# Sparse attention, compressed branch: the weighing of values by one plain fp32 product, or by rounded halves in two

## What is computed

```python
def nsa_attention(h, w_in, ...):
    ...
    n_cmp = (seq - CMP_LEN) // CMP_STRIDE + 1
    v_cmp = compress(vc_blk, pe_v, cv_w1, cv_w2)
    ...
        s_c = jnp.einsum("bgrtd,bgnd->bgrtn", qn, k_cmp) * scale
        p_c = masked_softmax(s_c, cmp_end[None, :] <= pos[:, None])
        o_c = jnp.einsum("bgrtn,bgnd->bgrtd", p_c.astype(v_cmp.dtype), v_cmp)
    ...
        return gt[..., 0:1] * o_c + gt[..., 1:2] * o_s + gt[..., 2:3] * o_w
```

## Time and profile before

| | |
|---|---|
| median of 3 executions | 2837.31 us (2834.18 to 2837.42) |
| the profiled execution | 2838.05 us, its span 2836.3 us |
| TensorE busy | 2756.7 us, 97% |
| VectorE busy | 1632.0 us, 58% |
| ScalarE busy | 1191.4 us, 42% |
| POOL busy | 239.7 us, 8% |
| granted TensorE clock, mean | 0.994 |

### The profile page before, as it was taken

The page is one execution under the profiler, slowest core; times in us unless marked ns, Lnnn a source line. Parts: engine busy times, 40 slices in busy tenths (PEclk is TensorE's granted clock), DMA queues, the critical chain, the costliest instruction groups (busy, mean ns, idle before and its releaser), DMA issues.

```text
span 2836.3 us, 34122 instructions
## 1 busy us (share of the span) xinstructions
PE 2756.7 (97%) x11756; PEld 2076.8 (73%) x11756; DVE 1632.0 (58%) x2240; ACT 1191.4 (42%) x1920; POOL 239.7 (8%) x246
## 2 busy tenths in 40 slices
PE   8999999999999989999999999999988999999999
PEld 6777776888877656888876667888866555788887
DVE  4444336777245766777338975554366666555532
ACT  4333234444234554444336654333234666433321
POOL 0000030000000003000005800000000333000000
PEclk9999999999999999999999999999999999999999
DMA  4222232333323112333231213333333000233323
GB/s 146 75 75 74 77 93 76 89 96 94 91 82 90 52 45 74 89 96 96 87 91 47 66 56 93 95 90 93 94 97 102 27 16 23 82 92 93 96 89 96
DMA packets 421253, 229.35 MB, mean 81 GB/s; under 512 B 8036, under 2 KB 413613, under 8 KB 421037
## 3 DMA queue, kind: packets, MB, share of 16 engines
q1 hardware_dynamic: 418700, 224.39, 27.2%
q10 hardware_dynamic: 2464, 3.81, 0.4%
HBM read 226.07 MB, written 2.10 MB: 80 GB/s over the span
## 4 chain that ended last, share of the span: by engine, by line
PE 85%; DVE 8%; ACT 4%; issue 2%; POOL 1%; DMA 0%; ACTq 0%; DVEq 0%; POOLq 0%
PE lin L815 22%; PE lin L817 22%; PE lin L816 22%; PE att L1126 1%; PE lin L1178 1%; PE att L1010 1%; DVE w_both L2197 1%; PE att L974 1%; PE att L973 1%; PE att L975 1%; ACT w_both L1525 1%; POOL con_p L776 1%; PE lin L1166 1%; PE stat L837 1%; PE trp L1143 1%
## 5 line engine op out<-in xcount | busy, mean ns | idle before, releaser
L2197 DVE TENSOR_TENSOR w_both<-raw,w_both 128x1024 fp32r<-128x1024 f32 x423 | 523.4, 1237 | 551.6 <-ACT w_both L1525 537.3
L815 PE MATMUL lin<-xh,w_both 128*128 128x512 f32 x1856 | 744.2, 401 | 10.3 <-DVE w_both L2197 10.0
L816 PE MATMUL lin<-xl,w_both 128*128 128x512 f32 x1856 | 735.8, 396 | 0.0
L817 PE MATMUL lin<-xh,w_both 128*128 128x512 f32 x1856 | 735.5, 396 | 0.0
L1525 ACT ACTIVATE w_both<-raw 128x1024 fp32r<-128x1024 f32 x423 | 448.2, 1059 | 664.5 <-PE lin L817 574.4
L815 PEld LDWEIGHTS lin<-xh,w_both 128*128 128x128 f32 x1856 | 349.5, 188 | 105.3 <-issue 20.1
L816 PEld LDWEIGHTS lin<-xl,w_both 128*128 128x128 f32 x1856 | 349.6, 188 | 87.0 <-issue 3.4
L817 PEld LDWEIGHTS lin<-xh,w_both 128*128 128x128 f32 x1856 | 349.6, 188 | 85.8
L815 PE MATMUL lin<-ffn_hi,w_both 128*128 128x512 f32 x704 | 280.1, 398 | 0.0
L817 PE MATMUL lin<-ffn_hi,w_both 128*128 128x512 f32 x704 | 279.1, 396 | 0.0
L816 PE MATMUL lin<-ffn_lo,w_both 128*128 128x512 f32 x704 | 279.1, 396 | 0.0
(11 more groups left out here) (450 smaller groups left out, 3759.4 us busy)
## 6 DMA issues: line engine op xcount, KB each, us to landing
raw<-in_ffn_w_up SPq DMA_DIRECT2D x176, 512.0 KB, 3.8
raw<-in_ffn_w_down SPq DMA_DIRECT2D x64, 512.0 KB, 3.8
raw<-in_a_w_in SPq DMA_DIRECT2D x48, 512.0 KB, 3.8
raw<-in_ffn_w_down SPq DMA_DIRECT2D x32, 384.0 KB, 3.3
raw<-in_conv_w_pw SPq DMA_DIRECT2D x24, 512.0 KB, 3.9
raw<-in_nsa_w_in SPq DMA_DIRECT2D x21, 512.0 KB, 3.7
raw<-in_a_w_out SPq DMA_DIRECT2D x16, 512.0 KB, 3.9
raw<-in_w_kv SPq DMA_DIRECT2D x16, 512.0 KB, 3.8
```

What stands on the lines that cost most here:

```text
L815: pe.matmul(bank, w_hi[s][:, k, :], h, start=start and k == 0, stop=False)
L816: pe.matmul(bank, w_hi[s][:, k, :], l, start=False, stop=False)
L817: done = pe.matmul(bank, w_lo[s][:, k, :], h, start=False, stop=stop and k == kc - 1)
L2197: dve.tensor_tensor(w_lo[s][:, :, :], raw[s][:, :, :], w_hi[s][:, :, :].bitcast(F32), ALU.subtract).then_inc(lo_done[s], 1)
```

## The change

The turned compressed weights and the compressed values are each split into a rounded high half and the rest. Of weights `w = wh + wl` and values `v = vh + vl` the products `vh wh`, `vh wl` and `vl wh` are made. The first two share one matmul: `pct` now has `wh` in its rows 0 to 61 and `wl` in rows 64 to 125 (`VC_LOW` = 64), and `vc_hh` has `vh` at both places; the rows 62 and 63 between are cleared. The third is a matmul of 62 rows with `vc_lo`, which lies in the memory of `x_sum`. ScalarE writes `wh` where it wrote the plain copy, and `vh` twice; VectorE makes `wl` (`compressed_low`, in its step 4 of each pair, behind the rotation) and once `vl`. TensorE waits for both writers of `pct` (`n_pc` counts two a pair). VectorE frees the bank of the compressed values, which ScalarE did.

```diff
--- before.py
+++ after.py
@@ -136,6 +136,8 @@
 NPARAM = _at
 PARAM_TILES = (NPARAM + P - 1) // P
 
+
+VC_LOW = 64
 
 CONST_AT = {}
 _at = 0
@@ -236,6 +238,7 @@
         xh = sb("xh", [P, DC, T], F32R)
         xl = sb("xl", [P, DC, T], F32R)
         dif_sm = sb("dif_sm", [P, 32])
+        x_sum_at = -(-nc.sbuf_base // 32) * 32
         x_sum = sb("x_sum", [P, T])
 
         def c_(name):
@@ -353,7 +356,7 @@
         v_all = m.place("v_all", [P, TB, 2, NG * HD])
         kc_bd = m.place("kc_bd", [P, NG, 2 * NCMP])
         vc_pre = m.place("vc_pre", [P, NG, 2 * NCMP])
-        vc_bd = m.place("vc_bd", [2 * NCMP, NG, P])
+        vc_hh = m.place("vc_hh", [VC_LOW + 2 * NCMP, NG, P], F32R)
         gates = m.place("gates", [P, TB, 3 * NH])
         n_raw = m.place("n_raw", [P, 2, T])
         n_t = m.place("n_t", [P, 2, T])
@@ -378,7 +381,8 @@
         n_e = m.place("n_e", [P, 2, 2, T])
         n_pt = m.place("n_pt", [P, 2, TB, T])
         ce = m.place("ce", [P, 2, TB, 2 * NCMP])
-        pct = m.place("pct", [2 * NCMP, T])
+        pct = m.place("pct", [VC_LOW + 2 * NCMP, T], F32R)
+        vc_lo = nc.alloc_sbuf_tensor_at("vc_lo", [2 * NCMP, NG, P], F32R, offset=x_sum_at)
         n_max, n_den, n_inv = (n_sm[:, k:k + 2 * s].rearrange("p (s h) -> p s h", h=2) for k, s in ((0, 2), (4, 2), (8, 3)))
 
         def n_exp(n, hh, w):
@@ -1151,10 +1155,12 @@
                     done.then_inc(n_tc, 1)
 
                 def weigh_compressed(p, bo):
-                    pe.wait_ge(n_pc, p + 1)
+                    pe.wait_ge(n_pc, 2 * p + 2)
                     if p == 0:
-                        pe.wait_ge(n_vcb, 1)
-                    pe.matmul(lin[bo][:, :], vc_bd[:, p // 2, :], pct[:, :], start=True, stop=False)
+                        pe.wait_ge(cleared, 4 + 2 * run[4])
+                        pe.wait_ge(n_vcb, 3)
+                    pe.matmul(lin[bo][:, :], vc_hh[:, p // 2, :], pct[:, :], start=True, stop=False)
+                    pe.matmul(lin[bo][:, :], vc_lo[:, p // 2, :], pct[0:2 * NCMP, :], start=False, stop=False)
 
                 def dense(k, unit, bank, hi, lo, last_pair=False):
                     (us, ut), (ub, ubt) = unit, bank
@@ -1902,9 +1908,10 @@
 
                 exps(0)
                 act.wait_ge(n_vct, 1)
-                act.activation(vc_bd[:, :, :], lin[vc_bank][0:2 * NCMP, :].rearrange("p (g n) -> p g n", g=NG), ACT.Copy).then_inc(n_vcb, 1)
-                act.wait_ge(n_vcb, 1)
-                act.sem_inc(bank_free[vc_bank], 1)
+                act.wait_ge(cleared, 4 + 2 * run[4])
+                for half in range(2):
+                    act.activation(vc_hh[half * VC_LOW:half * VC_LOW + 2 * NCMP, :, :],
+                                   lin[vc_bank][0:2 * NCMP, :].rearrange("p (g n) -> p g n", g=NG), ACT.Copy).then_inc(n_vcb, 1)
                 exp_compressed(0)
                 for p in range(NH // 2):
                     last_pair = p == NH // 2 - 1
@@ -1934,7 +1941,7 @@
                             act.wait_ge(n_tc, p + 1)
                             if p:
                                 act.wait_ge(n_pv, 2 * p - 1)
-                            act.activation(pct[:, :], lin[bo][0:2 * NCMP, :], ACT.Copy).then_inc(n_pc, 1)
+                            act.activation(pct[0:2 * NCMP, :], lin[bo][0:2 * NCMP, :], ACT.Copy).then_inc(n_pc, 1)
                     before = bo
                 place(8 * (NH // 2) - 1)
                 high_out(NH // 2 - 1, before)
@@ -2542,6 +2549,8 @@
 
                 dve.memset(kc_bd[:, :, :], 0.0).then_inc(cleared, 1)
                 dve.memset(vc_pre[:, :, :], 0.0).then_inc(cleared, 1)
+                dve.memset(vc_hh[VC_LOW // 2:VC_LOW, :, :].bitcast(F32), 0.0).then_inc(cleared, 1)
+                dve.memset(pct[VC_LOW // 2:VC_LOW, :].bitcast(F32), 0.0).then_inc(cleared, 1)
                 dve.tensor_scalar(q_gain[:, 0:1], col("nsa_q_norm_2"), HD ** -0.5, None, ALU.mult).then_inc(q_g, 1)
                 dve.wait_ge(rs_ready, rss.next())
                 for n in range(2):
@@ -2618,11 +2627,11 @@
                 scaled_out(g_raw[:, :], n_gr, 1)
                 split_next()
                 s, t = split_next()
-                b, _t = banks.take()
+                vc_bank, _t = banks.take()
                 dve.wait_ge(unit_done[s], t + 1)
                 for half in range(2):
                     r = slice(half * HD, half * HD + HD)
-                    done = dve.tensor_copy(vc_pre[r, :, half * NCMP:(half + 1) * NCMP], lin[b][r, 0:NC].rearrange("p (g n) -> p g n", g=NG))
+                    done = dve.tensor_copy(vc_pre[r, :, half * NCMP:(half + 1) * NCMP], lin[vc_bank][r, 0:NC].rearrange("p (g n) -> p g n", g=NG))
                 done.then_inc(n_vc, 1)
 
                 unseen = n_tabs[:, 2 * T + TB * NP32:].rearrange("p (b n) -> p b n", b=TB)[:, :, 0:NCMP]
@@ -2669,6 +2678,11 @@
                     dve.wait_ge(n_cg, p + 1)
                     dve.tensor_tensor(eights(p), eights(p), c_den.unsqueeze(2).broadcast_to([P, 8, NCMP]), ALU.mult).then_inc(n_cw, 1)
 
+                def compressed_low(p, bo):
+                    dve.wait_ge(n_pc, 2 * p + 1)
+                    dve.tensor_tensor(pct[VC_LOW:VC_LOW + 2 * NCMP, :], lin[bo][0:2 * NCMP, :], pct[0:2 * NCMP, :].bitcast(F32),
+                                      ALU.subtract).then_inc(n_pc, 1)
+
                 def low_out(p, bo):
                     dve.wait_ge(n_o, p + 1)
                     dve.tensor_tensor(att_lo[:, p, :], lin[bo][:, :], att_hi[:, p, :].bitcast(F32), ALU.subtract).then_inc(n_lo, 1)
@@ -2682,6 +2696,11 @@
                 dve.reciprocal(gates[:, :, :], gates[:, :, :]).then_inc(n_gate, 1)
                 top(1)
                 compressed_top(0)
+                dve.wait_ge(n_vcb, 2)
+                dve.tensor_tensor(vc_lo[:, :, :], lin[vc_bank][0:2 * NCMP, :].rearrange("p (g n) -> p g n", g=NG),
+                                  vc_hh[0:2 * NCMP, :, :].bitcast(F32), ALU.subtract).then_inc(n_vcb, 1)
+                dve.wait_ge(n_vcb, 3)
+                dve.sem_inc(bank_free[vc_bank], 1)
                 dve.wait_ge(n_gate, 2)
                 for p in range(NH // 2):
                     last_pair = p == NH // 2 - 1
@@ -2705,7 +2724,9 @@
                                 rotated_q(p + 1)
                             if i == 7:
                                 compressed_top(p + 1)
-                    bo, _t = banks.take()
+                        if i == 4:
+                            bo, _t = banks.take()
+                            compressed_low(p, bo)
                     before = bo
                 low_out(NH // 2 - 1, before)
                 residual_out(1, None, final, ("ffn_norm_g_2", DC))
```

## The result

The changed kernel takes 2849.97 us (median of 5 runs, 2849.6 to 2851.5); the kernel before takes 2837.31 (5 runs, 2834.18 to 2838.21). The ratio is 1.0047 [1.0037, 1.0058]: 12.7 us slower. The direction is the one that was forecast. The size is not: 7.7 us was forecast, and the time lies 1 us above the range.

The account below looks back on a forecast made before the run. TensorE, busy 97% of the span, was taken to bound the kernel. Six pairs at 1.02 us (6.1), pair 6 (2.2) and pair 7 (-0.6) sum to 7.7, on 2837.3 giving 2845.0 us; range 2838.5 to 2849.0.

Parts of the forecast that it names:

- What bounds and where the wait comes: Attention pairs: TensorE bounds; the subtraction queued behind VectorE's rotation makes it wait about 1.3 us, about 2.4 in pair 6.
- VectorE's terms: Subtraction behind the rotation: start 0.72 us after the last rotation instruction's start, 0.69 long, TensorE restarting 0.06 later.
- The choice between 0.61 and 0.72: Subtraction's start behind that of L2604: 0.61 us if unheld, 0.72 if the changed output partition holds it; 0.72 taken.
- TensorE's terms: Two products replacing the plain one: 0.33 + 0.23 + 0.09 us after the wait; TensorE alone saves 0.59 a pair.
- rival 3: Clock falls in the new waits: once gives 2846.5 us, in all seven pairs 2855.5; chance of the many 0.04.
- Pair 6: No dense product ahead of L1157, so TensorE arrives early and the first weighing comes 2.2 us later.
- Cover for others: VectorE's added 0.7 us delays a reciprocal and a maximum, but POOL and ScalarE have enough cover: cost 0.
- the once-only work: Extra rounding copy, low half of the values, bank release and two clearing instructions fall into idle time: cost 0.
- Rival 1: Between L1178 and the next L1157 other waits absorb about half the delay: +3.9, 2841.2 us; chance 0.16.
- rival 2: Subtraction ends before TensorE arrives, so all eight pairs keep the saving: -4.8, 2832.5 us; chance 0.08.
- Rival 4: New products no cheaper than the plain one, each 1.05 us: +1.5 a pair over the forecast, 2857 us; chance 0.01.

Follow-up runs that it names:

- low_first: The changed kernel with VectorE's subtraction for the low half made ahead of the rotation, not behind it: 2834.26 us, ratio 0.9989.
- plain_wait: The kernel before, plain product kept, with TensorE waiting for an added subtraction behind the rotation whose result is unused: 2853.52 us, ratio 1.0061.
- plain_sub: The kernel before with an added VectorE subtraction behind the rotation that nobody waits for, its output partition alternating between pairs: 2836.96 us, ratio 1.0001.
- rows: The changed kernel with the third product over 126 rows, vc_lo cleared below row 62, subtraction still behind the rotation: 2846.07 us, ratio 1.0032.
- plain_rows: The kernel before with its plain product over 128 rows in place of 62, vc_bd and pct cleared below row 62: 2837.22 us, ratio 0.9998.
- the filling: The changed kernel with unused plain products put ahead of TensorE's wait, one in pairs 0 to 5, two in pair 6: 2848.35 us, ratio 1.0035.
- low_first_rows: The changed kernel with both the subtraction ahead of the rotation and the third product over 126 rows: 2833.49 us, ratio 0.9985.

## Why the prediction was right in direction and short in size

**What bounds and where the wait comes: right.** The subtraction behind the rotation holds TensorE's queue up; the wait is 1.34 us in mid stage (1.3 forecast) and 2.29 in pair 6 (2.4). With the subtraction moved (low_first) nothing of the loss is left; with the wait alone (plain_wait) all of it comes.

**VectorE's terms: right.** Start behind the rotation 0.73 (0.72), subtraction 0.68 (0.69), TensorE's restart 0.06 (0.06). The choice between 0.61 and 0.72 is settled by plain_sub.

**TensorE's terms: one was mis-sized.** The step from L1162 to L1184 was put at 0.33 + 0.23 + 0.09 = 0.65 and measures 0.42 + 0.43 = 0.85. Both products behind the wait pay for a bare load. I took the steps from the earlier trace rows, where the loads all have 128 rows, and granted one change of 0.09 for the type. The type was the wrong feature; the rows count, and with the rows padded (rows) the step is 0.66. Where L1163's load has 62 rows it starts together with its matmul, and the load ahead of it, of 126 rows behind 128, goes in 0.23 us early. The last pair of the kernel after shows both with no wait in play:

```profile
2414.85 0.40 PE L1174 MATMUL lin<-att_hi,w_both 128*128 128x512 f32 x1
2414.86 0.19 PEld L1162 LDWEIGHTS lin<-pct,vc_hh 126*128 126x128 f32 x1
...
2415.09 0.39 PE L1162 MATMUL lin<-pct,vc_hh 126*128 126x512 f32 x1
2415.41 0.18 PEld L1163 LDWEIGHTS lin<-pct,vc_lo 62*128 62x128 f32 x1 [0.36 <-issue]
2415.41 0.50 PE L1163 MATMUL lin<-pct,vc_lo 62*128 62x512 f32 x1
2415.84 0.20 PEld L1184 LDWEIGHTS lin<-n_pt,v_all 128*64 128x64 f32 x4 [0.25 <-issue]
```

This is 0.2 us in each of the seven pairs with a wait, and pair 7 saves 0.39 and not 0.59: 1.6 us of the miss of 5.0. The kernel before paid the same twice a pair (1.37 = 0.32 + 1.05 in the earlier trace rows, 1.18 in plain_rows), and I had read its 0.32 as a matter of the type. The Trainium skill (TensorE: Matmul & The Clock Gate, section "LDWEIGHTS (loading the stationary operand)") says that a load's time goes by its columns and not by its rows. The loads' own records agree (0.18 us for 62 rows, 0.19 for 126): what costs here is not the length of the load but its start.

**The clock: the step that failed.** The forecast's case left it at 1.00 in all pairs and so put the falls at nothing in the sum; rival 3 named one fall as possible, with pair 6 as its place, and all seven as unlikely. Two came, 1.7 us each where that rival had 1.5: 3.4 us, the larger part of the miss. Two readings were wrong. The stretch of 2 us between 2386 and 2388, of which TensorE is busy 0.51 us, was taken as proof that such a gap is harmless. In the trace it is one idle of 1.49 us:

```profile
2387.91 0.63 PE L1143 MATMUL trp<-const,n_e 128*128 128x128 f32 x4 [1.49 <-ACT n_pt L1893]
```

So it said nothing of pair 6's 2.3, and one gap is one throw: behind pair 6's idle of some 2.3 us the clock fell in all four traces without the filling (the kernel after twice, plain_wait, rows) and in none of two with it. And behind the 1.3 to 1.4 us of a pair in mid stage it fell in some pairs, one of six in the kernel after (the same one twice), two of six in plain_wait, none in rows. By these runs pair 6's fall belonged in the sum, and one or two more in the range. With both corrections the sum is 7.7 + 1.6 + 3.4 = 12.7; with one of them alone the time would have stayed inside the range (2845.0 + 3.4 = 2848.4, or 2846.6).

**Pair 6: right** (2.4 for 2.2; the 0.2 is the term above). **Cover for others: right,** as far as these times tell. ScalarE, POOL and the once-only work cost nothing that shows: low_first has them all and is faster than before. **Rival 1** (absorbed) and **rival 2** (in time) did not come; rival 2 is what low_first makes of it, by the order and not by luck. **Rival 4** is excluded by the saving in low_first (0.75 from L1162 to the weighing, where two dear products would take 2.1).

## What to carry to other kernels

A cheaper product on the bounding engine is worth its price only if its new input is ready: look where the producer's queue puts it, and try the order first. Here one block of three lines moved past the rotation turned +12.7 us into -2.9. When a wait of a microsecond or two is put in front of TensorE, price the clock's fall behind it too, for each wait. And look at the rows of the weight loads on both sides: padding 62 rows to 126 or 128 with zeros saved 0.19 us between products of 128 rows, and cost 0.19 behind one of 64.

## What the runs showed of the hardware that I had not expected

A weight load of 62 rows beside loads of 126 or 128 rows is not taken in ahead of its matmul: its matmul starts 0.32 instead of 0.24 us behind the last one, and the first weighing product 0.43 instead of 0.32 behind it, 0.19 us together in low_first against low_first_rows, and the same 0.19 for the plain product (plain_rows). Behind loads of 64 rows it is the load of 62 that is taken in early (0.43 us), and those of 126 and 128 are not (low_first and plain_rows, pair 6). Whether the 64-column weighing load adds to the second number was not tried apart.

The granted clock fell to about a half (0.52 and 0.53 in the stretches shown) behind idles of 1.3 us that in other pairs of the same kernel left it at 1.00, and did so in the same pair in both traces of that kernel. The length of the idle does not decide alone: the wait of 1.42 us in front of the next dense products stands in all eleven traces, and the clock stays at 1.00 behind it in every one. Each fall cost 1.6 to 1.7 us. Filling part of the idle took away the falls behind the waits, and a fall appeared elsewhere, in pair 7, also twice. What decides between two equal waits stays open.
